# TensorE's order in the MoBA and stick-breaking attention units: values of the preceding unit ahead of the transpositions of the present one

## The reference, cut to what matters

```python
# MoBA, per chunk of 128 queries and per head (with 2 blocks, all past keys are selected)
logits = q @ k.T * ATTN_SCALE + bias          # NEG_INF where a key is not seen
p = softmax(logits)                           # 128 x (128 .. 512)
out = p @ v

# stick-breaking, per block of 128 queries and per head
z = q @ k.T * scale
log1m = where(mask, log_sigmoid(-z), 0)
after = cumsum(log1m, reverse=True) - log1m
out = where(mask, exp(log_sigmoid(z) + after), 0) @ v
```

## Time and profile before

| | |
|---|---|
| Median of three runs | 1833.1 us |
| Profiled execution: its own time | 1834.32 us |
| Profiled execution: its span | 1832.5 us |
| TensorE (PE) busy | 1793.8 us, 98% |
| VectorE (DVE) busy | 1096.0 us, 60% |
| ScalarE (ACT) busy | 740.7 us, 40% |
| GpSimd (POOL) busy | 130.6 us, 7% |
| moba stage | about 131 to 177 us of the span |
| sb units | about 1327 to 1386 us |
| dsa units after them | to about 1426 us |

### The profile page before, as it was taken

One profiled execution on the slowest core, in us unless ns is written; L12 is line 12 of the kernel. 1 busy time (PEld: TensorE's weight loads), 2 busy tenths in 40 slices (PEclk: granted clock), 3 DMA queues, 4 the chain that ended last, 5 costly groups with the idle time before them and its releaser, 6 DMA issues.

```text
span 1832.5 us, 23391 instructions
## 1 busy us (share of the span) xinstructions
PE 1793.8 (98%) x8864; PEld 1445.9 (79%) x8864; DVE 1096.0 (60%) x1647; ACT 740.7 (40%) x1061; POOL 130.6 (7%) x123
## 2 busy tenths in 40 slices
PE   7999999999999999999999999999999999999998
PEld 5885788888888787778888888887856888888887
DVE  6998444444433676554766773337997467666423
ACT  4237443333323225554444442322257444445321
POOL 1000100000011110731000000100000100000000
PEclk9998999999999999999999999999999999999999
DMA  5320222232232521112322223233310223322232
GB/s 194 126 93 24 69 92 92 97 109 92 92 115 92 160 82 47 51 42 92 107 100 92 92 95 112 92 128 93 107 47 1 69 92 99 107 92 92 95 112 69
DMA packets 27687, 167.39 MB, mean 91 GB/s; under 512 B 3499, under 2 KB 5675, under 8 KB 8801
## 3 DMA queue, kind: packets, MB, share of 16 engines
q1 hardware_dynamic: 23840, 157.13, 25.1%
q0 software_dynamic: 1920, 6.42, 1.2%
q10 hardware_dynamic: 1856, 2.85, 0.6%
HBM read 161.93 MB, written 2.13 MB: 90 GB/s over the span
## 4 chain that ended last, share of the span: by engine, by line
PE 91%; DVE 6%; ACT 1%; issue 1%; DMA 0%; DVEq 0%; ACTq 0%
PE ps L440 26%; PE ps L441 26%; PE ps L442 26%; PE ps L681 2%; PE ps L633 2%; PE ps L652 2%; DVE ring L1605 1%; PE ps L453 1%; PE ps L455 1%; PE ps L454 1%; DVE ring L1597 1%; DVE score L1810 1%; PE ps L717 0%; DVE w_lo L1310 0%; PE ps L719 0%
## 5 line engine op out<-in xcount | busy, mean ns | idle before, releaser
L440 PE MATMUL ps<-a_hi,w_hi 128*128 128x512 f32 x1608 | 633.9, 394 | 6.8 <-DVE a_lo L1316 3.8
L441 PE MATMUL ps<-a_lo,w_hi 128*128 128x512 f32 x1608 | 626.9, 390 | 0.0
L442 PE MATMUL ps<-a_hi,w_lo 128*128 128x512 f32 x1608 | 626.9, 390 | 0.0
L440 PEld LDWEIGHTS ps<-a_hi,w_hi 128*128 128x128 f32 x1608 | 302.5, 188 | 83.9 <-issue 18.6
L441 PEld LDWEIGHTS ps<-a_lo,w_hi 128*128 128x128 f32 x1608 | 302.5, 188 | 63.2 <-issue 1.7
L442 PEld LDWEIGHTS ps<-a_hi,w_lo 128*128 128x128 f32 x1608 | 302.4, 188 | 63.1
L1310 DVE TENSOR_TENSOR w_lo<-raw,w_hi 128x2048 fp32r<-128x2048 f32 x80 | 188.2, 2352 | 216.3 <-ACT w_hi L896 215.9
L896 ACT CAST w_hi<-raw 128x2048 fp32r<-128x2048 f32 x79 | 150.4, 1904 | 300.0 <-PE ps L442 259.7
L440 PE MATMUL ps<-h_hi,w_hi 128*128 128x512 f32 x516 | 200.7, 389 | 0.0
L441 PE MATMUL ps<-h_lo,w_hi 128*128 128x512 f32 x516 | 200.7, 389 | 0.0
L442 PE MATMUL ps<-h_hi,w_lo 128*128 128x512 f32 x516 | 200.7, 389 | 0.0
(11 more groups left out here) (248 smaller groups left out, 2004.0 us busy)
## 6 DMA issues: line engine op xcount, KB each, us to landing
raw<-weights_dram SPq DMA_DIRECT2D x146, 1024.0 KB, 4.9
bias_t<-bias_rows_scratch POOLq DMA_DIRECT2D x8, 256.0 KB, 4.9
ncb<-decay_rows_scratch POOLq DMA_DIRECT2D x8, 256.0 KB, 5.4
xT<-x_in_dram ACTq DMA_DIRECT2D x4, 256.0 KB, 5.2
xT<-x_in_dram SPq DMA_DIRECT2D x4, 256.0 KB, 4.8
raw<-weights_dram SPq DMA_DIRECT2D x2, 512.0 KB, 7.8
out_dram<-xT SPq DMA_DIRECT2D x4, 256.0 KB, 2.1
v<-pT POOLq DMA_DIRECT2D x1, 1016.0 KB, 6.6
```

Of the source, the lines that this page charges most:

```text
L440: pe.matmul(dst, wh, hi[:, k0 + k, :], start=start and k == 0, stop=False)
L441: pe.matmul(dst, wh, lo[:, k0 + k, :], start=False, stop=False)
L442: last = pe.matmul(dst, wl, hi[:, k0 + k, :], start=False, stop=stop and k == nk - 1)
```

## The change

In TensorE's loop, values of unit `i-1` are issued before turn of unit `i` where unit `i-1` is moba or sb. Nothing is added or removed, and the queues of the other engines are as before.

```diff
+                    ahead = 1 <= i <= n and run[i - 1].kind in ("moba", "sb")
+                    if ahead:
+                        values(run[i - 1])
                     if 0 <= i < n:
                         turn(run[i])
-                    if 1 <= i <= n:
+                    if 1 <= i <= n and not ahead:
                         values(run[i - 1])
```

## The result

| | before | after |
|---|---|---|
| Median | 1832.37 us (1831.29 to 1834.27, 11 runs) | 1837.0 us (1836.2 to 1838.56, 11 runs) |
| Profiled execution: its own time | 1834.32 us | 1836.23 us |
| Profiled execution: its span | 1832.5 us | 1834.4 us |

The ratio of after to before is 1.0025, with a 95% interval of 1.0017 to 1.0033. The change makes the kernel 4.6 us slower, by the medians. The profiled execution of after is one of its quicker ones: seven of the eleven runs lie between 1836.2 and 1837.1, and four between 1838.3 and 1838.6.

What follows compares the result with a forecast made beforehand. VectorE was taken to bind the moba and sb stages, TensorE the dsa units. Moba 2.5 us (tail 2.0, VectorE held up 0.5) plus sb 0.4 gave 2.9 us on the median of 1833.1: 1836.0 us, range 1832.6 to 1839.7.

Steps and rivals of the forecast that it cites:

- What bounds the stages: Moba and sb stages: VectorE binds both, so shorter TensorE waits for `pr` in the middle gain 0.
- 1.18 us per round: Moba middle: a round takes VectorE 9.71 us and gapless TensorE 8.53, so TensorE can lose 1.18 unseen.
- VectorE held up in moba: Moba: later turn and copy delay the exponentials VectorE needs; 0.5 us lost, bounds 0 and 1.09.
- slack of 0.92 us: Moba: exponentials of unit 7 end at 151.16 us, VectorE asks at 152.08; a 1.09 us delay would lose 0.17.
- Moba tail at the full clock: Last moba steps: uncovered copy waits put the end of values of unit 15 at 177.28 against 176.67, 0.6 us later.
- The same low stretch again in moba: Moba tail: the half-rate TensorE stretch recurs after idle time, costing 1.4 us, making the tail 2.0 us.
- rival A: Only the full-clock part, half-rate stretch shorter or hidden, VectorE not held up: 0.9 us, 1834.0; chance 0.17.
- line 776 near 179: Sign in the profile after: line 776, following the moba tail, would start near 179 us.
- sb passage: Passage from sb to dsa: values of unit 14 wait for the second copy, 0.4 us later; bounds -1.1 and +1.2.
- rival C: Moba tail: low clock holds through line 776, doubling its 3.70 us at most: 6.6 us, 1839.7; chance 0.19.
- B: Faster: turn's 7.7 us of sb waits for `pr` are real and values fill them: 1825.4; chance 0.04.
- D: Slower by ScalarE: copies stand behind exponentials, steps wait 0.8 us, rounds 2.0 above VectorE's: 1842; chance 0.10.

Runs made afterwards that it cites:

- e3: New order kept in the middle of both stages, old order in their last steps, against the kernel before: 1831.51 us, ratio 0.9996.
- g1: Kernel before with the 16 convolution taps of the moba stage on 8 of 512 columns, relieving VectorE: 1829.52 us.
- g2: Changed kernel with the 16 convolution taps of the moba stage on 8 of 512 columns, relieving VectorE: 1834.60 us.
- e1: New order in the moba stage alone, sb as in the kernel before: 1834.11 us, ratio 1.0009 to before.
- g3: Kernel before with the new order only in steps 15 and 16 of the sb and dsa run: 1832.46 us, ratio 0.9997.
- e2: New order in the sb units alone, moba as in the kernel before: 1834.18 us, ratio 1.0004 to before.
- e4: Kernel before with the new order only in the last steps (moba 14 and 15, sb 15 and 16): 1836.77 us, ratio 1.0021.
- h1: Kernel before with one ScalarE swap in the moba tail, copies of unit 13 ahead of the exponentials of unit 15: 1831.76 us, ratio 0.9993.
- f3: New order mid-stage, old order in last steps, plus four unused matmuls ahead of turn of unit 14: 1832.48 us, ratio 1.0000 to before.
- f2: Kernel before plus four unused matmuls ahead of turn of unit 14 in the moba tail: 1831.52 us, ratio 0.9997.
- e0: The changed kernel, unaltered, run once more beside the kernel before: 1836.07 us, ratio 1.0016.

## Why the prediction was right, and where not

The forecast was 1836.0 us, on before's median of 1833.1; measured were 1837.0 and, once more, 1836.07, against 1832.4. As a difference, 2.9 us was forecast and 4.6 and 3.7 were measured. The first lies just past the 3.7 us from which the prediction speaks of slower, the second on it. The two profiled executions are nearer than that, 1.9 us apart, and there the split is the other way round: the forecast gave moba 2.5 and sb 0.4, measured were 0.33 and 1.68. What bounds the stages and the chain of the tail held; the terms of the clock stood at the wrong stage.

- **What bounds the stages.** Right, and shown three ways: VectorE's 32.13 of 33 us and 36.52 of 37, unchanged; e3, where the new order in the middle costs nothing; g1, where less work for VectorE shortens the stage. The waits for `pr` that vanished (10.6 and 7.7 us in the two stretches, weight loads and matmuls together) gained nothing. The 1.18 us per round that TensorE was said to have to give away do cover the 0.47 us per round that g1 and g2 lay open.
- **VectorE held up in moba, +0.5.** Wrong, measured 0. From the first scores to the last reciprocal of VectorE it is 170.91 - 131.22 = 39.69 us after and 39.70 before. The slack of 0.92 us was read rightly, and nearly used up, but not passed: in after the exponentials of unit 7 end at 151.55 + 0.20 = 151.75 us, and VectorE asks for them at 151.84. The sum took one whole values, 1.09, for the delay; it was 0.83.

```profile
151.55 0.20 ACT L1090 ACTIVATION_READ_ACCUMULATOR ring<-ring,stat 128x1 f32 x1
```

```profile
151.84 0.17 DVE L1614 RECIPROCAL stat<-stat 128x2 f32<-128x2 f32 x1
```

- **Moba tail at the full clock, +0.6 against the profile before.** This was 2.0 against a tail of before without the half rate (177.28 against 176.67 - 1.40); measured 9.06 - 7.30 = 1.76. The 1.40 for the low clock of before was right. Of the difference, 0.13 lies in the chain from values of unit 13 to line 776, 176.84 - 170.99 = 5.85 us where the sum had 177.28 - 171.30 = 5.98. Another 0.14 is the start of that chain: values of unit 13 begin 0.67 us after the first copy (170.32 in after's ScalarE timeline), where the sum had 0.50 + 0.31 = 0.81. Probably the sum set the two copies end to end, while they overlap: the two of width 512 behind them take 1.07 us together and one alone 0.59. The waits in it came out as 0.68 and 0.78 us for the 0.67 and 0.83 of the sum.
- **The same low stretch again in moba, +1.4.** Not in either profile of after, nor in e1: the clock was full there, so the tail went as rival A has it. The sign named for it, line 776 near 179, failed: it starts at 176.84. The four slower runs of after (1838.3 to 1838.6) would fit a tail with it, but no trace of such a run exists.
- **sb passage, +0.4, bounds -1.1 to +1.2.** The full-clock part was near: 82.83 - 82.52 = 0.3 for 0.4 (g3). The size of the whole was not: 85.06 - 82.52 = 2.5 us against the passage at the full clock, and 1.7 against before's own. The upper bound looked only at ScalarE's queue. It should have doubled the work that follows, as rival C did for moba: the low level now runs on through turn of unit 15 and the scores of unit 19, behind which VectorE resumes after 1.76 us. This term is the one that was mis-sized most.
- **The end.** At the full clock the sum is 1.76 + 0.3 = 2.1 us, which is what the order itself costs. e1, with the moba part alone, came out 1.2 above before, e2 1.3. The rest of the 3.7 to 4.6 us, 1.6 to 2.5 us, is put down to the clock: the passage gives 85.06 - 82.83 = 2.2 in a profile, and what before loses to its own low stretches has to come off. The sum isn't closed, as it mixes medians with single profiles. The forecast's 2.9 came near the result with one stretch of low clock that didn't come back (1.4), one that was taken as unchanged and grew, and a term for VectorE that was nothing (0.5). That the total fits is partly luck.
- **Rivals.** B fell with g1 and g2. D fell: VectorE's busy share did not drop, and the one wait inside a round is 0.29 us in after (0.28 in g2), under the 0.3 us from which it decides. C's mechanism is real and decided nothing at its own place in after, but it did in e4 (4.2 us) and, at a place it hadn't named, in after's sb passage.

What stays open is how often each stretch falls to the low level. In the profiles with the moba tail idle for 1.80 us or more ahead of unit 13's values or unit 14's turn (before, e2, g3, e4) three of four show the low level, and in the eight with 1.46 us or less none does. In the passage it is six of seven with 1.70 to 1.81 us (not e3) and three of seven with 1.23 us (before, h1 and g1), g1 and g2 counted. That points to longer waits as the cause, but it is one trace per kernel. before, e2 and g3 have the same 1.80 us in the moba tail and differ, and e3 and f3 have the same 1.81 and 0.72 us in the passage and differ, so the wait alone doesn't decide, and I show no more than the tendency. What the middle steps of the sb stage do to the first of these waits was shown by g3's 1.23 us. That they alone cost e3 nothing fits with the granted clock of its runs: eight of eleven have 0.996 or 0.997 over the span, against 7 of the 33 of before beside it. The profiled executions with neither stretch (e1, e3, f2, g3) have 0.995 to 0.997, the others of the table 0.992 to 0.995. e4's profiled execution lies 0.5 us above its median, but how many of its runs hold the long stretch isn't known.

## What to carry to other kernels

Before reordering an engine to shorten its waits, ask which engine sets the pace of the stage: the waits for VectorE fell here from 10.6 + 7.7 to 1.9 + 0.3 us without any gain, and new ones for the copies came in their place. A loop that hands work to another engine and takes it back pays for a short distance between the two where nothing else covers it: in its last steps (1.76 us here), and in each round once that engine sets the pace (0.47 us). Keep the longest distance there, or give the tail an order of its own. And price every added gap of TensorE twice, once as idle time and once as the half rate that may follow it, including the work behind it that another engine waits for.

## What the runs showed of the hardware

- **Low clock after gaps of one to two microseconds.** I had not expected the low level to last from 171.5 to 182 us in e4, after a wait of 1.98 us and through groups of matmuls broken only by two waits of 0.68 us. Its price there, 4.2 us, is twice what the order itself costs.
- **The hand-over.** TensorE starts values 0.68 us after the end of turn of unit 14 and 0.78 after that of unit 15, and of that a copy of 384 takes 0.43 us and one of 512 takes 0.59. So the two hand-overs together are 0.25 and 0.19 us, and the forecast's 0.05 + 0.19 = 0.24 held.
- **The same kernel in levels.** After's runs gather at 1836.2 to 1837.1 and 1838.3 to 1838.6 us, at granted clocks of 0.993 or 0.994 and 0.992 over the span. A difference of 0.001 in a mean clock over 1834 us is 1.8 us of full rate. The upper group did not come back in e0, whose runs have two at 1833.1 and 1833.3 us (clock 0.995) and nine at 1835.6 to 1837.1.
